# A two-layer hybrid decoder trunk on one core: the residual stream kept transposed, the RMS factor applied behind the projections

## What is computed

```python
for l in range(2):
    hn = rms_norm(x, norm_mix[l])
    x = x + (even_mixer if l == 0 else odd_mixer)(hn, ...)
    x = x + hier_moe(rms_norm(x, norm_ffn[l]), ...)
# even mixer: proj = hn @ w_in -> a_q, a_f, a_i, a_g, b_q, b_k, b_v, b_low (16 columns), b_r
#   two chunked gated linear attentions (f = lb + (1-lb)*sigmoid(a_f); b's gate from b_low @ gla_w_up)
#   head norms, silu gates, @ w_out
# odd mixer: proj = hn @ w_in -> c_q, c_k (rope), c_v, c_g, d_x, d_gate
#   retention beside conv(4) + RG-LRU scan on d_x, @ w_out
# hier_moe: one of 4 groups, then top 2 of its 8 experts; an expert is (silu(h @ w1) * (h @ w3)) @ w2
```

## Time and profile before

| | us |
|---|---|
| median of three runs | 1178.65 |
| the profiled execution | 1177.77 |
| its span, first to last instruction | 1176.0 |
| PE busy | 884.2 (75%) |
| weight load of PE busy | 540.1 (46%) |
| DVE busy | 342.1 (29%) |
| ACT busy | 304.9 (26%) |
| mean granted clock | 0.937 |
| read from HBM | 441 MB, 376 GB/s over the span |

### The profile page before, as it was taken

One profiled execution on the slowest core, in us unless ns is written; L12 is line 12 of the kernel. 1 busy time (PEld: TensorE's weight loads), 2 busy tenths in 40 slices (PEclk: granted clock), 3 DMA queues, 4 the chain that ended last, 5 costly groups with the idle time before them and its releaser, 6 DMA issues.

```text
span 1176.0 us, 25056 instructions
## 1 busy us (share of the span) xinstructions
PE 884.2 (75%) x10181; PEld 540.1 (46%) x10188; DVE 342.1 (29%) x815; ACT 304.9 (26%) x520; POOL 13.1 (1%) x17
## 2 busy tenths in 40 slices
PE   7999997776666766666688998777667666676675
PEld 5988853333333333333348886343333333333333
DVE  4798841111111111111126884111111111111112
ACT  4655641121101101101023854112110110110102
POOL 3000000000000000000000000000000000000000
PEclk9999999998889889999999999999998899988989
DMA  9643589999999999999995378999999999999996
GB/s 333 247 144 144 206 367 388 428 428 428 429 429 428 430 429 429 428 429 428 428 404 205 144 312 350 403 430 429 428 429 428 428 429 429 428 428 429 427 428 274
DMA packets 45682, 442.67 MB, mean 376 GB/s; under 512 B 3712, under 2 KB 4880, under 8 KB 20176
## 3 DMA queue, kind: packets, MB, share of 16 engines
q1 hardware_dynamic: 45376, 441.41, 90.3%
q10 hardware_dynamic: 144, 0.52, 0.1%
q0 software_dynamic: 128, 0.26, 0.1%
HBM read 441.13 MB, written 1.05 MB: 376 GB/s over the span
## 4 chain that ended last, share of the span: by engine, by line
DMA 53%; PE 36%; ACT 4%; DVE 3%; issue 2%; SPq 1%; POOL 0%; DVEq 0%; ACTq 0%
DMA weights<-in_moe_w_dram 52%; PE bank L990 11%; PE bank L621 3%; PE bank L623 3%; PE bank L622 3%; PE bank L1004 3%; PE sums_of_x L621 2%; PE bank L968 2%; PE sums_of_x L622 1%; PE sums_of_x L623 1%; PE sums_of_x L1013 1%; PE sums_of_x L786 1%; DMA weights<-in_even_w_in_dram 1%; ACT w_hi L1106 1%; DVE w_lo L1384 1%
## 5 line engine op out<-in xcount | busy, mean ns | idle before, releaser
L990 PE MATMUL bank<-weights,gates 128*32 128x256 f32 x4096 | 291.4, 447 | 126.3 <-DMA weights<-in_moe_w_dram 116.2
L990 PEld LDWEIGHTS bank<-weights,gates 128*32 128x32 f32 x4096 | 147.8, 128 | 254.6 <-DMA weights<-in_moe_w_dram 120.9
L1004 PE MATMUL bank<-weights,gates 128*32 128x256 f32 x2048 | 123.8, 382 | 85.9 <-DVE gates L1776 62.1
L1774 DVE TENSOR_TENSOR gates<-gates,bank 128x128 f32<-128x128 f32 x64 | 18.4, 288 | 416.9 <-ACT gates L1048 416.9
L1004 PEld LDWEIGHTS bank<-weights,gates 128*32 128x32 f32 x2048 | 62.7, 109 | 147.0 <-issue 87.1
L1048 ACT ACTIVATE gates<-bank 128x128 f32<-128x128 f32 (+1 forms) x66 | 18.9, 287 | 410.1 <-PE bank L990 410.1
L1770 DVE TENSOR_TENSOR gates<-bank,vecs 128x256 f32<-128x256 f32 x64 | 27.2, 425 | 268.2 <-PE bank L977 268.2
L1013 PE MATMUL sums_of_x<-gates 32*128 32x256 f32 x1024 | 73.3, 400 | 31.2 <-ACT gates L1275 31.2
L1384 DVE TENSOR_TENSOR w_lo<-weights,w_hi 128x2048 fp32r<-128x2048 f32 (+1 forms) x32 | 73.3, 2290 | 29.6 <-ACT w_hi L1106 29.4
L968 PE MATMUL bank<-tok,gates 128*32 128x256 f32 x1024 | 68.5, 385 | 16.3 <-issue 10.1
L1013 PEld LDWEIGHTS sums_of_x<-gates 32*128 32x128 f32 x1024 | 46.2, 184 | 63.4 <-ACT gates L1275 62.0
(11 more groups left out here) (277 smaller groups left out, 1019.0 us busy)
## 6 DMA issues: line engine op xcount, KB each, us to landing
weights<-in_moe_w_dram SPq DMA_DIRECT2D x186, 2048.0 KB, 35.2
weights<-in_even_w_in_dram SPq DMA_DIRECT2D x6, 2048.0 KB, 14.0
weights<-in_moe_w_dram SPq DMA_DIRECT2D x12, 1024.0 KB, 34.6
weights<-in_odd_w_in_dram SPq DMA_DIRECT2D x5, 2048.0 KB, 33.2
weights<-in_even_w_in_dram SPq DMA_DIRECT2D x2, 1024.0 KB, 10.4
weights<-in_even_w_out_dram SPq DMA_DIRECT2D x1, 2048.0 KB, 7.6
weights<-in_even_w_out_dram SPq DMA_DIRECT2D x2, 1024.0 KB, 4.8
weights<-in_odd_w_out_dram SPq DMA_DIRECT2D x1, 2048.0 KB, 7.7
```

The costliest lines, as they stand in the source:

```text
L990: ins = pe.matmul(bank[6][PASS * j:PASS * (j + 1), 0:T], got_T[:, k % 2, k // 2, :], up[:, k, :, j * P:(j + 1) * P], start=(k == 0), stop= ...
L1004: ins = pe.matmul(bank[7][PASS * q:PASS * (q + 1), T:2 * T], hid_T[:, c, :], down[:, c, q * T:(q + 1) * T], start=(c == 0), stop=(c == Q - 1),
```

## The change

- The residual stream lies transposed (`x_T`, in the bytes of `x`; the sum after a mixer goes to `act_T`). In layer 0, x is turned raw, as it comes from memory; in layer 1 the experts of layer 0 sum x^T in PSUM banks 4 to 7 directly, starting from `act_T` (`begin_sums`), and the scatter matmul has its operands exchanged for it. The experts' own tiles move to banks 0 to 3.
- Projections run from raw x^T times norm_mix. The token's factor comes later: as a row (`row`, the same on all partitions) multiplied by DVE into a_f, a_q, b_q, b_k, the low rank, d_x, the rope tables and d_gate; as a per-token scale in ACT's copy or silu for a_i, b_v, a_g, b_r, c_v, c_g.
- The first two steps run chunk by chunk: rounding, remainder and 12 matmuls for each of 8 chunks of 128 channels (`first_channels`, `split_first`). POOL's part is gone.
- norm_mix comes as columns for the new order of channels, by 16 small loads a layer (`norm_columns`): layer 0's issued by ACT first of all, layer 1's by SP behind b_v. `vecs` is loaded in two parts, behind a_q and a_i; a_q is loaded in halves, a_f and d_x in three parts; the load of w_rg waits until the masks are in.
- b_low is no step of its own: 16 fp32 matmuls of 32 columns, four groups side by side (`low_rank`). w_up is loaded four times over into a cleared tile.
- The output projection makes x^T: 48 matmuls of 256 columns. Squares go to PE as matmuls with a column of ones; ACT copies normalised tokens no more but turned raw ones, and the factor goes into the expert's pick matrix.

```diff
-SPLIT = ("a_f", "even_out1", "odd_out0")
+SPLIT = ("a_f", "a_q", "d_x", "even_out1", "odd_out0")
...
+        def norm_columns(eng, l):
+
+            src = vectors[:, KC * l:KC * (l + 1)].rearrange("(k h) n -> h n k", h=P // KC)
+            for h in range(P // KC):
+                eng.dma_start(w_cols[KC * h:KC * (h + 1), KC * l:KC * (l + 1)], src[h],
+                              allow_slow_non_contiguous=True).then_inc(w_cols_loaded, 16)
...
+            def first_channels(l):
+
+                for k in range(KC):
+                    _, lo, hi = first_piece(l, k)
+                    pe.wait_ge(*first_lo.at(l, k + 1))
+                    pe.wait_ge(act_rest, KC * l + k + 1)
+                    for m in range(4):
+                        cols = slice(m * P, (m + 1) * P)
+                        ins = three(bank[m][:, 0:T], hi[:, cols], lo[:, cols], act_hi[:, k, :], act_lo[:, k, :],
+                                    k == 0, k == KC - 1)
+                    if k % 4 == 3:
+                        ins.then_inc(step_done.sem, 1)
...
+            def low_rank():
+
+                w = work(LOW_AT, KC * P).rearrange("p (k c) -> p k c", k=KC)[:, :, 0:LOW]
+                pe.wait_ge(*is_loaded(piece_loaded["b_low"]))
+                for half in range(2):
+                    for part in (act_hi, act_lo):
+                        for j in range(Q):
+                            k = half * Q + j
+                            ins = pe.matmul(bank[0][LOW * j:LOW * (j + 1), 0:T], w[:, k, :], part[:, k, :].bitcast(F32),
+                                            start=(half == 0 and part is act_hi), stop=(half == 1 and part is act_lo),
+                                            tile_position=(0, LOW * j), skip_group_check=True)
...
+            def out_pair(l, i, g, first, last):
+
+                name, _, lo, hi = step_parts(l, i)
+                for c in range(2):
+                    for j in range(2):
+                        k = 4 * int(name[-1]) + 2 * STEPS[l][i - 1][2] + j
+                        at = j * D + (2 * g + c) * P
+                        ins = three(bank[OUT_BANKS[l][g]][:, c * T:(c + 1) * T], hi[:, at:at + P], lo[:, at:at + P],
+                                    y_hi[:, k, :], y_lo[:, k, :], first and c == 0 and j == 0, last and j == 1, shared=True)
+                return ins
...
+                group(2)
+                pe.wait_ge(w_folded, l + 1)
+                logits_of(0)
+                logits_of(1)
+                group(3)
+                logits_of(2)
+                pe.wait_ge(*squares_added.at(l, 1))
+                norms_of(0, True, False)
+                logits_of(3).then_inc(logits_ready.sem, 1)
+                pe.wait_ge(*squared.at(2 * l + 1, 4))
+                norms_of(3, False, True).then_inc(sums_ready.sem, 1)
                 turn(0)
...
+                first_channels(0)
+                pe.wait_ge(*raw_kept.at(0, 4))
+                pe.wait_ge(*norms_set.at(0, 2))
+                pe.matmul(bank[ROW_BANK][:, T:2 * T], const("ones"), sumsq, start=True, stop=True).then_inc(row_ready.sem, 1)
+
+                def row_is_read(m):
+                    if m == 3:
+                        pe.wait_ge(*row_read.at(0, 1))
+
+                by_channel(0, 3, range(4, 8), row_is_read)
+                by_channel(0, 4, range(4, 8))
+                pe.wait_ge(af_kept, 1)
...
+                def begin_sums(b):
+
+                    for k in (2 * (b - X_BANK), 2 * (b - X_BANK) + 1):
+                        if l == 0:
+                            pe.matmul(chunk_in_bank(k), ident, act_T[:, k, :], start=(k % 2 == 0), stop=True, skip_group_check=True)
...
-            keep_warm(22, 0)
+            keep_warm(16, 0)
             pe.wait_ge(ident_loaded, 16)
-            turn_tokens(0)
-            keep_warm(12, 0)
+            turn_tokens()
+            keep_warm(8, 0)
             even_mixer()
             route(0)
             experts(0)
-            keep_warm(26, 5)
-            turn_tokens(2)
-            keep_warm(5, 0)
             odd_mixer()
...
+                for g in range(4):
+                    act.wait_ge(*x_added.at(l, g + 1))
+                    f(pair_of(squares, g), pair_of(act_T, g), ACT.Square).then_inc(squared.sem, 1)
+                norm_root(2 * l + 1)
+                for t, (a, h) in enumerate(GROUPS):
+                    act.wait_ge(*x_turned.at(l, t + 1))
+                    act.copy(tok[:, a, :].rearrange("p (k c) -> p c k", k=KC)[:, 64 * h:64 * h + 64, :],
+                             bank[TURN_BANKS[l][t]][:, :].rearrange("p (c k) -> p c k", k=KC)).then_inc(x_kept.sem, 1)
...
-                round_step(0, 3)
-                act.wait_ge(*step_done.at(0, 2))
-                for m in range(4):
-                    f(kA[:, m * T:(m + 1) * T], bank[m][:, 0:T], ACT.Sigmoid).then_inc(sig_done, 1)
-                for i in (4, 5):
-                    round_step(0, i)
+                act.wait_ge(af_kept, 1)
+                f(kA, kA, ACT.Sigmoid).then_inc(sig_done, 1)
+                round_step(0, 4)
...
+            norm_columns(act, 0)
+            square_tokens()
+            first_hi_of(0, (0, 1))
+            norm_root(0)
+            first_hi_of(0, (2, 3))
+            for b in (2, 3):
+                for k in (2 * b, 2 * b + 1):
+                    chunk_hi(0, k)
+                first_hi_of(0, (2 * b, 2 * b + 1))
+            for b in range(Q):
+                keep_raw(0, b)
+            round_step(0, 3)
...
+            scatters = experts(0)
+            first_hi_of(1, range(4))
+            act.wait_ge(scattered, scatters)
+            for b in (2, 3):
+                for k in (2 * b, 2 * b + 1):
+                    chunk_hi(1, k)
+                first_hi_of(1, (2 * b, 2 * b + 1))
+            round_step(1, 3)
+            for b in range(Q):
+                keep_raw(1, b)
+                act.wait_ge(*raw_kept.at(1, b + 1))
+                f(pair_of(squares, b), pair_of(x_T, b), ACT.Square).then_inc(squared.sem, 1)
...
+            def split_first(l):
+
+                dve.wait_ge(w_cols_loaded, (l + 1) * 16 * P // KC)
+                for b in range(2):
+                    pair_hi(l, b)
+                    for k in (2 * b, 2 * b + 1):
+                        chunk_lo(l, k)
+                        first_lo_of(l, k)
+                    if l == 0 and b == 0:
+                        norm_mean(0)
+                if l == 0:
+                    token_scale()
+                for k in range(KC // 2, KC):
+                    chunk_lo(l, k)
+                    first_lo_of(l, k)
...
-                dve.wait_ge(sig_done, 4)
+                dve.wait_ge(*row_ready.at(0, 1))
+                dve.tensor_copy(row, bank[ROW_BANK][:, T:2 * T]).then_inc(row_read.sem, 1)
+                dve.wait_ge(*row_read.at(0, 1))
+                dve.wait_ge(*step_done.at(0, 2))
+                tt(kA.rearrange("p (m t) -> p m t", m=4), low_banks[:, :, 0:T], row.unsqueeze(1).to_broadcast([P, 4, T]),
+                   ALU.mult).then_inc(af_kept, 1)
+                rest_step(0, 4)
...
                 dve.wait_ge(aq_kept, 4)
+                tt(qA.rearrange("p (m t) -> p m t", m=4), qA.rearrange("p (m t) -> p m t", m=4),
+                   row.unsqueeze(1).to_broadcast([P, 4, T]), ALU.mult).then_inc(aq_scaled, 1)
+                dve.wait_ge(*step_done.at(0, 5))
+                tt(low, bank[0][:, 0:T], row, ALU.mult).then_inc(low_kept, 1)
+                dve.wait_ge(aq_scaled, 1)
...
                 gap_A(2)
                 rest_step(0, 8)
+                dve.wait_ge(bqk_kept, 4)
+                for v in (qB, kB):
+                    v = v.rearrange("p (m t) -> p m t", m=2)
+                    tt(v, v, row.unsqueeze(1).to_broadcast([P, 2, T]), ALU.mult).then_inc(bqk_scaled, 1)
                 keep_A(0)
                 softplus()
                 for l in range(2):
...
+                rest_step(1, 3)
                 mark(dve.memset(dx[:, :, 0:3], 0.0))
-                dve.wait_ge(vector_step, steps[0])
-                for i in (3, 4):
-                    rest_step(1, i)
+                dve.wait_ge(*squared.at(2, 4))
+                dve.tensor_reduce(sumsq, squares.rearrange("p k t -> p t k"), AX.X, ALU.add).then_inc(norms_set.sem, 1)
+                rest_step(1, 4)
+                dve.wait_ge(*row_ready.at(1, 1))
+                ts(sums[:, :], bank[ROW_BANK][:, 0:TT], 1.0 / D, EPS, ALU.mult, ALU.add).then_inc(mean_set.sem, 1)
+                ts(row, bank[ROW_BANK][:, T:2 * T], 1.0 / D, EPS, ALU.mult, ALU.add).then_inc(row_read.sem, 1)
+                dve.wait_ge(*rooted.at(2, 1))
+                dve.reciprocal(scale[:, :], root[:, :]).then_inc(scale_ready.sem, 1)
+                link(dve.reciprocal(row, row))
+                dve.wait_ge(dx_kept, 4)
+                link(tt(dx[:, :, 3:3 + T], dx[:, :, 3:3 + T], row.unsqueeze(1).to_broadcast([P, 4, T]), ALU.mult))
```

545 lines of the change are left out of this document (278 added, 267 removed).

## The result

The changed kernel is slower: 1192.6 us median (1192.06 to 1195.07, 4 runs) against 1178.7 us (1177.57 to 1179.08, 4 runs) for the kernel before on the same chip, a ratio of 1.0125 [1.0109, 1.0141]. The prediction was 1177.2 us, 1171.5 to 1182.5. The profiled execution has a span of 1193.2 us, 17.2 more than the 1176.0 of before.

A forecast was written before the change was run, and what follows sets the result against it. The chain of waits was read as 53% DMA (expert loops, unchanged) and 36% PE (mixers). Layer 0 +3.6 us and the odd mixer -5.05 sum to -1.45, giving 1177.2 us as a median, range 1171.5 to 1182.5.

The forecast's parts named there:

- Landing of the small loads: Start of layer 0: norm_columns' data arriving up to 3 us after the last issue was taken as hidden.
- the late-start rival: Start: small loads issue slower or land after 12 us, delaying all of layer 0; +4.6 us, 1181.8; chance 0.15.
- (a): Even mixer: the row factor multiplies a_f on DVE before ACT's sigmoid and rounding; PE stalls 3.0 us before step 4.
- (b): Even mixer: low rank as 16 fp32 matmuls on four column groups instead of 24; 1.0 us saved on PE.
- step 3: Layer 0's start, first half of a_q: begins at 25.0 us instead of 30.55.
- step 4: Even mixer, the projection step after step 3: starts at 33.8 us, behind DVE's remainder.
- (c): Even mixer: DVE waits for b_q and b_k copies, with diagonal, softplus, folds queued behind; PE stalls 3.1, then 1.9 us.
- the 5.5 us lead of the start: Start of layer 0: step 3 was to begin 5.5 us earlier than before.
- Step 9 to M: Even mixer, from step 9's start to its last residual add (M): +0.7 for wider out-projection steps, +1.1 for the last.
- Exit: Layer 0, from the mixer's last residual add through the router's counts to the first expert: +0.6 us.
- The clock rival: Even mixer: PE's clock dips after idle stretches; two dips give +3.0 us, 1180.2; chance 0.15.
- Odd mixer: Layer 1, from layer 0's last scatter (its end is S): gate matmuls at S + 29.1, before 36.6; 5.05 us gained overall.

## Why the prediction was wrong, step by step

**Landing of the small loads.** This is the step that failed first: "its landing has no row; up to 3 us after the last issue is hidden". It took 9.4 us. I had the mechanism, and its place and its start of effect (3.8 us), in the late-start rival with a chance of 0.15; I priced it from the issue time, which was right within 1 us (7.33 against 6.4), while the landing had no row. A cost without a row needs a wide bound, and its rival more weight, when it stands ahead of everything. Measured: 7.2 us at M.

**(a) and (b).** Right. With one load, step 3, step 4 and its stall were 0.6, 0.3 and 0.5 us off. Two sums of the start don't close as written: its terms give the first rounding's end at 11.4, not 11.6, and VectorE's split 9.5 us and more, not the 9.2 from 11.6 to 20.8 (measured 10.2, 17.55 to 27.77); both are inside the 0.6.

**(c), the wait with 6.5 us queued behind it.** Right in its waits: step 7's end + 10.2 and + 14.9 (forecast 10.3 and 15.0), 4.1 us in all as the reordering shows, where I had 5.0. Two things were missed. 2.1 us of clock came on top. And I booked the stall against the 5.5 us lead of the start, "+1.2 net"; when the lead went, the stall was paid in full.

**Step 9 to M.** Forecast +1.8. Eight kernels whose clock stayed up show 90.5 us here against 88.13, +2.4: the last step has 3.54 us between its last two adds (two pairs of logits between them) where before had 1.82, so +1.7 in place of +1.1. The changed kernel took 92.55, the clock again.

**Exit.** M + 11.5 was forecast for the counts and is what four profiles at full clock show (11.50 to 11.52). With the clock down it is 12.7 to 14.4, and where the clock fell after the counts the first expert took 11.2 us to N in place of 8.8. The forecast held for the clock it assumed, and in layer zero neither profile of the changed kernel had that clock.

**The clock rival** was named, with two dips and 3.0 us. The changed kernel's profile shows falls after the start's wait (0.78 from 20 to 30 us), after (c), at the exit, at the odd entry, at the gate matmuls and under layer one's first expert. What can be told apart is 2.1 us after (c), by an edit for that alone, and 2.9 us at the exit of layer zero, by comparing profiles whose clock fell there with profiles whose clock didn't. Its evidence against, that one idle stretch of 3.05 us left the clock full, was one case.

**Odd mixer.** First matmul right to 0.1 us. Step 3 at S + 15.3 in place of 13.7 and the gate matmuls at 32.3 in place of 29.1: two terms mis-sized, the strided reduction (3.81, not 2.2 "like a remainder") and a reciprocal of 256 columns (1.73, where I had 1.4 for the roots and both reciprocals together), and the clock. (The end of step 4 at S + 27.6 doesn't follow from its terms, which give 26.7; nothing else rests on it.) With filler and pairwise adds five profiles show the gate matmuls at S + 30.0 to 30.1 and S to M 100.1 to 100.2, a gain of 4.6 to 4.7 against 5.35 forecast. So the even and the odd sums were both near what the design gives; the changed kernel didn't get it: its clock fell behind its waits.

Put together for layer zero, 16.3 us over before where 3.6 were forecast: 7.2 landing, 2.1 clock after (c), 0.6 the wider last steps, 2.9 clock at the exit; 12.8 against the 12.7 to be explained. The terms come from different kernels, so a fit to 0.1 us is partly luck, but no large cause is missing. For layer one +0.9 in place of -5.05: the gate matmuls' 1.7 us and the entry's first chunks by the clock, 1.3 for the reciprocal (1.73 against an ordinary operation's 0.41), 0.7 for the reduction, M to N 1.3. How these 6 us divide was not settled beyond that.

Not settled: what decides where and in which execution the clock falls. After the same wait of 2.46 us the gate matmuls took 5.38 us in some of these kernels and 3.69 in others. Seven kernels with the odd mixer of the changed one, differing elsewhere, ran it in 101.5 to 104.1 us, and the filler moved the falls more surely than it removed them.

## What to carry to other kernels

A transposed vector is best stored transposed in the input: one load of 128 rows landed in 3.4 us, 1,024 single numbers 9.4 us after the last of their issues, and the wait for them stood ahead of all else. A wait put into an in-order queue costs what is queued behind it; take the unrelated work (softplus, folds, the copies not needed yet) ahead of or behind it, which gave 6.2 us here at one place (2.1 of it the clock's) and 1.8 us at full clock at another. A lead gained at the start should not be booked against a stall later on: price the stall as if the lead were not there.

## What the runs showed of the hardware

TensorE's clock was at its lower level for 3 to 8 us after waits of 1.9 to 7.4 us, and also at the exit, where TensorE is busy by the profile but, just before the fall, with matmuls of a single column and with ones whose weights are 36 columns wide. It was not so after every such wait or exit: the exit of layer zero ran below full clock up to the counts in 8 of the 16 profiles of the new kernels. A strided reduction of 2048 numbers to 256 took 3.81 us on VectorE, where contiguous adds of the same data take 0.69 for 512; a reciprocal of 256 columns took 1.73 us, four times an ordinary operation of that size. Sixteen loads of 64 single numbers took ScalarE 7.33 us to issue, 0.46 each; the other sixteen held SyncE for 12.26 us, 0.77 each, a step of the diff that I had not costed. Single numbers are not the reason for that: with rows of 32 bytes the same sixteen took 6.94 us on ScalarE and 14.58 on SyncE.
